# Attention scores in three rounded passes: queries, keys and rotary parts split into a high and a low part

## What is computed

```python
q = (rmsnorm(c_q, g_q) @ w_uq).reshape(B, T, N_HEADS, QK_NOPE + ROPE_DIM)
q_rope = rope(q[..., QK_NOPE:], pos)
k_rope = rope(k_r[:, :, None, :], pos)[:, :, 0, :]
q_lat = jnp.einsum('bthn,lhn->bthl', q_nope, w_uk)
s = (jnp.einsum('bqhl,bkl->bhqk', ql, ckv) + jnp.einsum('bqhr,bkr->bhqk', qr, krope))
p = jax.nn.softmax(jnp.where(mask, s * ATTN_SCALE, -jnp.inf), axis=-1)
```

## Time and profile before

| | us |
|---|---|
| median of 3 runs | 1477.38 |
| lowest, highest | 1475.58, 1477.49 |
| the profiled execution | 1478.73 |
| its span, first to last instruction | 1476.7 |
| TensorE busy / VectorE / ScalarE | 1283.9 / 532.7 / 457.6 |
| attention pairs, from the first scores | about 307.8 to 398 |
| granted TensorE clock, mean over the span | 0.937 |

### The profile page before, as it was taken

The page is one execution under the profiler, slowest core; times in us unless marked ns, Lnnn a source line. Parts: engine busy times, 40 slices in busy tenths (PEclk is TensorE's granted clock), DMA queues, the critical chain, the costliest instruction groups (busy, mean ns, idle before and its releaser), DMA issues.

```text
span 1476.7 us, 22967 instructions
## 1 busy us (share of the span) xinstructions
PE 1283.9 (87%) x8612; PEld 711.9 (48%) x8613; DVE 532.7 (36%) x1057; ACT 457.6 (31%) x713; POOL 32.9 (2%) x40
## 2 busy tenths in 40 slices
PE   6999999999999998888887788788788888888785
PEld 4999999887767753332232222222222323222222
DVE  4336446275574342322322232222223232232233
ACT  5432334245443223222222222222222322232223
POOL 1000000000100000000000000000000000000000
PEclk9999999999999989999899899889989989998988
DMA  9454551132354389999999999999999999999997
GB/s 325 142 171 139 167 168 41 36 109 78 118 163 150 134 340 393 428 430 433 430 435 431 430 432 430 436 430 432 432 429 402 424 433 432 429 436 430 433 431 287
DMA packets 70680, 474.45 MB, mean 321 GB/s; under 512 B 9628, under 2 KB 46752, under 8 KB 56432
## 3 DMA queue, kind: packets, MB, share of 16 engines
q1 hardware_dynamic: 69712, 472.35, 78.4%
q0 software_dynamic: 688, 1.43, 0.3%
q10 hardware_dynamic: 240, 0.09, 0.0%
HBM read 470.49 MB, written 3.38 MB: 321 GB/s over the span
## 4 chain that ended last, share of the span: by engine, by line
PE 63%; DMA 25%; DVE 6%; ACT 3%; issue 3%; DVEq 0%; ACTq 0%; SPq 0%
DMA ring<-in_w_down 14%; PE ps L955 11%; PE ps L974 8%; DMA ring<-in_w_up 7%; PE ps L653 5%; PE ps L655 5%; PE ps L654 5%; PE ps L929 3%; DVE hreg L1690 3%; PE ps L961 2%; DMA gate_b<-in_w_down 2%; DMA gate_b<-in_w_up 2%; PE ps L817 2%; PE ps L818 2%; PE ps L819 2%
## 5 line engine op out<-in xcount | busy, mean ns | idle before, releaser
L1690 DVE TENSOR_TENSOR hreg<-ps,hreg 128x512 f32<-128x512 f32 x264 | 160.9, 682 | 198.2 <-PE ps L981 198.2
L955 PE MATMUL ps<-ring,cq 128*32 128x512 f32 x1600 | 187.9, 611 | 24.9 <-DVE hreg L1690 18.4
L1694 DVE TENSOR_TENSOR work<-work,ps 128x128 f32 x33 | 9.5, 288 | 453.7 <-PE ps L961 453.7
L653 PE MATMUL ps<-xT_hi,w_hi 128*128 128x320 f32 (+1 forms) x528 | 165.2, 313 | 0.6 <-DVE w_lo L1395 0.6
L654 PE MATMUL ps<-xT_lo,w_hi 128*128 128x320 f32 (+1 forms) x528 | 164.2, 311 | 0.0
L655 PE MATMUL ps<-xT_hi,w_lo 128*128 128x320 f32 (+1 forms) x528 | 164.1, 311 | 0.0
L974 PE MATMUL ps<-ring,work 128*32 128x512 f32 x768 | 125.3, 812 | 18.5 <-DMA ring<-in_w_down 18.5
L981 PE MATMUL ps<-krt,const 32*128 32x512 f32 x528 | 102.7, 626 | 29.7 <-ACT krt L1341 29.7
L955 PEld LDWEIGHTS ps<-ring,cq 128*32 128x32 f32 x1600 | 52.0, 112 | 139.6 <-issue 129.0
L1395 DVE TENSOR_TENSOR w_lo<-ring,w_hi 128x1024 fp32r<-128x1024 f32 (+1 forms) x66 | 76.8, 1205 | 108.6 <-ACT w_hi L1091 108.6
L1091 ACT CAST w_hi<-ring 128x1024 fp32r<-128x1024 f32 (+1 forms) x66 | 65.2, 1033 | 146.8 <-PE ps L655 146.8
(11 more groups left out here) (306 smaller groups left out, 1650.9 us busy)
## 6 DMA issues: line engine op xcount, KB each, us to landing
ring<-in_w_up SPq DMA_DIRECT2D x23, 4096.0 KB, 31.8
ring<-in_w_down SPq DMA_DIRECT2D x23, 4096.0 KB, 32.7
ring<-in_w_gate SPq DMA_DIRECT2D x23, 4096.0 KB, 32.2
ring<-in_w_in SPq DMA_DIRECT2D x32, 1024.0 KB, 8.2
gate_b<-in_w_gate SPq DMA_DIRECT2D x8, 4096.0 KB, 31.0
gate_b<-in_w_up SPq DMA_DIRECT2D x8, 4096.0 KB, 31.8
gate_b<-in_w_down SPq DMA_DIRECT2D x7, 4096.0 KB, 33.1
ring<-in_w_o SPq DMA_DIRECT2D x16, 1024.0 KB, 7.2
```

The source lines that it names most:

```text
L653: pe.matmul(out, hi, xT_hi[:, c, :], start=c == 0, stop=False)
L955: last = pe.matmul(ps[r:r + B, bank, :], x[:, k % 4, k // 4, :], w[:, k, :], start=k < 4, stop=k >= KC - 4)
L1690: dve.tensor_tensor(h, ps[:, COMB_BANKS[u], :], h, ALU.add).then_inc(comb_added, 1)
```

## The change

Scores are formed in three fp32r passes, for the plain rows and for the rotary rows: six matmuls a step in place of two. Queries and keys get a high part (q_hi, k_hi; ScalarE copies) and a low part (q_lo, k_lo; VectorE subtractions), each in one buffer that all pairs use; the query banks are now emptied by VectorE, as the key banks already were. The rotary query is first rotated into att_a, then split (rope_hi_ready, rope_lo_ready). The rotary keys are split once, ahead of the pairs (krt_hi, krt_lo). Before its first pass of a pair, scores waits for rope_lo_ready. queries_hi(p+1) and keys_hi(p+1) move on ScalarE to behind the first key copy of pair p. In VectorE's keys(p), queries_lo(p+1) and keys_lo(p+1) keep their place, and the rotary subtraction stands behind them.

```diff
@@ psum_jobs @@
-        return ([(f"qr{p}", "act")] + [(f"q{2 * p + i}", "act") for i in range(2)]
+        return ([(f"qr{p}", "act")] + [(f"q{2 * p + i}", "dve") for i in range(2)]
@@ tensors @@
-        qt = r2[:, 0:1920].rearrange("p (b i t) -> p b i t", b=2, i=3)
-        kt = r2[:, 1920:4224].rearrange("p (b i k) -> p b i k", b=2, i=2)
+        q_hi = nc.alloc_sbuf_tensor_at("q_hi", [P, 3, T], F32R, offset=r2_at)
+        q_lo = nc.alloc_sbuf_tensor_at("q_lo", [P, 3, T], F32R, offset=r2_at + 4 * 960)
+        k_hi = nc.alloc_sbuf_tensor_at("k_hi", [P, 2, KEYS], F32R, offset=r2_at + 4 * 1920)
+        k_lo = nc.alloc_sbuf_tensor_at("k_lo", [P, 2, KEYS], F32R, offset=r2_at + 4 * 3072)
+        krt_hi = nc.alloc_sbuf_tensor_at("krt_hi", [P, KEYS], F32R, offset=work_at + 4 * 2560)
+        krt_lo = nc.alloc_sbuf_tensor_at("krt_lo", [P, KEYS], F32R, offset=krt_at)
@@ TensorE, scores(h) @@
-                q, k = qt[:, p % 2], kt[:, p % 2]
-                pe.wait_ge(q_ready, p + 1)
+                pe.wait_ge(krt_lo_ready, 1)
+                pe.wait_ge(rope_lo_ready, p + 1)
                 pe.wait_ge(drained["dve"], drain_count[f"K{h}_1"])
-                pe.wait_ge(drained["act"], drain_count[f"q{h}"])
+                rows = slice(64 * i, 64 * i + 64)
 
                 def score(out, t0, tn, k0, kn):
-                    pe.matmul(out, q[:, i, t0:t0 + tn], k[:, i, k0:k0 + kn], start=True, stop=False)
-                    return pe.matmul(out, q[64 * i:64 * i + 64, 2, t0:t0 + tn], krt[64 * i:64 * i + 64, k0:k0 + kn], start=False, stop=True)
+                    t, k = slice(t0, t0 + tn), slice(k0, k0 + kn)
+                    pe.matmul(out, q_hi[:, i, t], k_hi[:, i, k], start=True, stop=False)
+                    pe.matmul(out, q_hi[:, i, t], k_lo[:, i, k], start=False, stop=False)
+                    pe.matmul(out, q_lo[:, i, t], k_hi[:, i, k], start=False, stop=False)
+                    pe.matmul(out, q_hi[rows, 2, t], krt_hi[rows, k], start=False, stop=False)
+                    pe.matmul(out, q_hi[rows, 2, t], krt_lo[rows, k], start=False, stop=False)
+                    return pe.matmul(out, q_lo[rows, 2, t], krt_hi[rows, k], start=False, stop=True)
@@ ScalarE @@
             keys_hi(0)
+            act.wait_ge(ulast_ready, 1)
+            act.copy(krt_hi[:, :], krt[:, :]).then_inc(krt_hi_ready, 1)
...
                 for i in range(2):
                     act.wait_ge(psum_full, full(f"q{2 * p + i}"))
-                    drain("q", act.copy(qt[:, p % 2, i, :], bank(f"q{2 * p + i}")[:, 0:T]))
+                    act.copy(q_hi[:, i, :], bank(f"q{2 * p + i}")[:, 0:T]).then_inc(q_hi_ready, 1)
+                for i in range(2):
+                    for s, (k0, kn) in enumerate(((0, 256), (256, 320))):
+                        act.wait_ge(psum_full, full(f"K{2 * p + i}_{s}"))
+                        act.copy(k_hi[:, i, k0:k0 + kn], bank(f"K{2 * p + i}_{s}")[:, 0:kn]).then_inc(k_hi_ready, 1)
+                        if i == s == 0 and p + 1 < H // 2:
+                            queries_hi(p + 1)
+                            keys_hi(p + 1)
+                        if i == 0 and s == 1:
+                            act.wait_ge(q_ready, p + 1)
+                            act.copy(q_hi[:, 2, :], att_a).then_inc(rope_hi_ready, 1)
...
             queries(0)
-            queries_hi(1)
-            keys_hi(1)
...
-                if p + 2 < H // 2:
-                    queries_hi(p + 2)
-                    keys_hi(p + 2)
@@ VectorE @@
             keys_lo(0)
+            dve.wait_ge(krt_hi_ready, 1)
+            dve.tensor_tensor(krt_lo[:, :], krt[:, :], krt_hi[:, :].bitcast(F32), ALU.subtract).then_inc(krt_lo_ready, 1)
...
             def keys(p):
+                for i in range(2):
+                    h = 2 * p + i
+                    dve.wait_ge(q_hi_ready, h + 1)
+                    drain("q", dve.tensor_tensor(q_lo[:, i, :], bank(f"q{h}")[:, 0:T], q_hi[:, i, :].bitcast(F32), ALU.subtract))
                 for i in range(2):
                     for s, (k0, kn) in enumerate(((0, 256), (256, 320))):
                         name = f"K{2 * p + i}_{s}"
-                        dve.wait_ge(psum_full, full(name))
-                        drain(name, dve.tensor_copy(kt[:, p % 2, i, k0:k0 + kn], bank(name)[:, 0:kn]))
-                        if i == 0 and s == 1 and p + 1 < H // 2:
-                            queries_lo(p + 1)
-                            keys_lo(p + 1)
+                        dve.wait_ge(k_hi_ready, 4 * p + 2 * i + s + 1)
+                        drain(name, dve.tensor_tensor(k_lo[:, i, k0:k0 + kn], bank(name)[:, 0:kn], k_hi[:, i, k0:k0 + kn].bitcast(F32), ALU.subtract))
+                        if i == 0 and s == 1:
+                            if p + 1 < H // 2:
+                                queries_lo(p + 1)
+                                keys_lo(p + 1)
+                            dve.wait_ge(rope_hi_ready, p + 1)
+                            dve.tensor_tensor(q_lo[:, 2, :], att_a, q_hi[:, 2, :].bitcast(F32), ALU.subtract).then_inc(rope_lo_ready, 1)
                         if i == s == 0:
                             dve.wait_ge(drained["act"], drain_count[f"qr{p}"])
-                            rotate(qt[:, p % 2, 2, :], qraw, bank(f"qrot{p}")[:, 0:T], att_a, att_b, f"qrot{p}").then_inc(q_ready, 1)
+                            rotate(att_a, qraw, bank(f"qrot{p}")[:, 0:T], att_a, att_b, f"qrot{p}").then_inc(q_ready, 1)
```

More of the change, by code:

```diff
@@ L177, in trunk_layer_kernel @@
         cq = sb("cq", [P, LC, T])
+        krt_at = nc.sbuf_base
         krt = sb("krt", [P, KEYS])
+        assert nc.sbuf_base == krt_at + 4 * KEYS
         const = sb("const", [P, C_ALL])
@@ L182, in trunk_layer_kernel @@
         work = sb("work", [P, 4960])
+        work_at = nc.sbuf_base - 4 * 4960
         small = sb("small", [P, 64])
@@ L322, in trunk_layer_kernel @@
         wk_hi_ready, wk_lo_ready = sem("wk_hi_ready"), sem("wk_lo_ready")
+        q_hi_ready, k_hi_ready, rope_hi_ready, rope_lo_ready = sem("q_hi_ready"), sem("k_hi_ready"), sem("rope_hi_ready"), sem("rope_lo_ready")
+        krt_hi_ready, krt_lo_ready = sem("krt_hi_ready"), sem("krt_lo_ready")
         s_ones, first_half = sem("s_ones"), sem("first_half")
```

## The result

The changed kernel takes 1502.81 us (median of four runs, 1494.45 to 1508.86) against 1477.12 us for the kernel before (1475.58 to 1477.49): ratio 1.0175, 95% interval 1.0147 to 1.0202. It is slower, as forecast, but by 25.7 us and not by 6.2. The profiled execution took 1508.13 us (span 1506.1) against 1478.73 (span 1476.7): 29.4 us more.

A forecast was written before the change was run, and what follows sets the result against it. TensorE was taken to bound attention, passing delays on one for one. Terms 3.7 + 1.6 - 0.05 - 0.5 = +4.7 us, plus 1.5 for the clock, gave +6.2 us: 1483.6 us, range 1477.5 to 1489.5.

The forecast's parts named there:

- TensorE sets the pace of the stage, and a delay is passed on one for one: Attention stage: TensorE bounds it, VectorE close behind; any delay moves everything after it one for one.
- The worth of the passes, 0.5 us a pair: Scores on TensorE: three fp32r passes take 6.4 us a pair in place of 6.9, 2 us gained in all.
- 0.10 us of waiting plus an exposed load, 0.05 to 0.11: Score groups on TensorE: price of each change between 128 and 64 rows, six a head in both kernels.
- Rival B: Scores: row changes cost fp32r passes nothing, 4.6 us a pair, 1476.5 us in all; chance 0.10.
- rival D: Scores: narrow or 64-row fp32r passes run at f32 speed, +6 us more, about 1489 us; chance 0.05.
- The 1.8 us a head: Scores: estimate from the skill's issue-gap formula for six passes a step, set aside for 3.2 us a head.
- The first wait, 3.7 us: First pair: TensorE waits 3.7 us before the first scores for VectorE's added subtractions.
- Rival E: First scores: shorter or earlier side-engine work leaves a wait of 1 to 2 us, 1478 to 1481 us; chance 0.12.
- The gaps of pairs 1 and 2, +0.8 us a cycle, and pair 3: Before value matmuls: gaps of about 1.7 us, net +0.8 us for each of two cycles; third cycle net -0.05 us.
- rival A: Whole kernel: the clock doesn't fall, so only +4.7 us, 1482.1 us; chance 0.13.
- The clock, +1.5 us: First scores: one half-clock stretch of about 3.2 us follows TensorE's new wait and loses 1.5 us.
- Rival C: Pairs 1 and 2: clock also falls after one or both 1.7 us gaps, +1.6 us each, 1485 to 1487; chance 0.22.

The follow-up runs named there:

- experiment 1: Changed kernel with the first gap and the two gaps before attend filled by useless 512-column f32 matmuls on TensorE; 1482.60 us, ratio 1.0025.
- experiment 11: Changed kernel with the 1.7 us gaps filled, plus 24 fp32r passes of 256 columns in three forms before the first scores; 1483.84 us, one run.
- experiment 7: Kernel before with only its f32 score matmuls reordered, two changes of rows a head in place of six; 1474.67 us, ratio 0.9977.
- experiment 10: Changed kernel with 32 useless fp32r matmuls of 512 columns between the first gap and the first scores; 1503.68 us, ratio 1.0169.
- Experiment 8: Changed kernel with only the first gap, ahead of the first scores, filled by useless matmuls; 1498.26 us, ratio 1.0139.
- experiment 3: Changed kernel with next-pair weight casts behind the last key copy and weight subtractions behind the drains of transposed probabilities; 1478.78 us, ratio 1.0004.
- experiment 5: Changed kernel with the next pair's weight work moved later and score passes grouped to two changes of rows a head; 1469.97 us, ratio 0.9955.
- experiment 2: Changed kernel with each score step again two f32 matmuls, waits, splits and order kept; 1512.51 us, ratio 1.0219.
- experiment 6: Changed kernel with later weight work, grouped passes, and four of eight convolution scalings moved behind the first two heads' maxima; 1469.41 us, ratio 0.9946.
- experiment 4: Changed kernel with only its score passes reordered, two changes of rows a head in place of six; 1498.32 us, ratio 1.0117.

## Why the prediction was right, and where it failed

**TensorE sets the pace of the stage, and a delay is passed on one for one.** Right: 28.6 of 29.4 us are there when the output projection begins.

**The worth of the passes, 0.5 us a pair.** Right: 6.4 us for the last pair of the changed kernel, the only one at full clock, against 6.9. At full clock, in experiment 1, the groups of a head stand in the chain like this:

```profile
335.66 0.26 PE ps L778
...
337.16 0.32 PE ps L781
337.48 0.12 PE ps L782
337.59 0.12 PE ps L783
337.71 0.29 PE ps L778
338.00 0.15 PE ps L779
338.15 0.15 PE ps L780
...
338.88 0.26 PE ps L778
...
391.37 0.42 PE ps L831
```

The 256-column rotary group is 0.32 + 0.12 + 0.12 = 0.56 (forecast 0.56), the 320-column group behind it 0.29 + 0.15 + 0.15 = 0.59 (0.58), and a head, from 335.66 to 338.88, 3.22 us (3.2). The term "0.10 us of waiting plus an exposed load, 0.05 to 0.11" for a change of rows is 0.15 to 0.21, and experiment 11 measures 0.19. Rival B (changes cost passes nothing) falls by the same number, and rival D (narrow passes at f32 speed) by the groups. For the f32 matmuls of the kernel before, the prediction's reading was too simple: experiment 7 saves four changes a head and gains 0.40 us, 0.10 for each, not 0.20. The Trainium skill, TensorEngine Tiling (Array Packing), Key Properties, says that a changed tiling mode drains the engine; the trace agrees for rows (0.31 us against 0.12) and shows no such cost for weight columns from 128 to 64 (0.12 against 0.12). The 1.8 us a head that the prediction worked out from the Trainium skill, TensorE: Matmul & The Clock Gate, Back-to-back issue gap, is far off, but the page gives that formula for a matmul by itself and says that it counts too little for narrow ones in a stream with weight loads; the trace has 3.2 us with six changes of rows and 2.5 with two.

**The first wait, 3.7 us.** Right: 3.48. Of the single steps, the pair of query subtractions is 0.80 us to its successor in line (0.82) and the three of the weights 2.87 (2.87, 308.47 to 311.34). Rival E falls. (Its time was priced loosely: a wait of 1 to 2 us in place of 3.7 takes 1.7 to 2.7 us from 1483.6, and 1.5 more if the clock stays up, so 1479.4 at the lowest and not 1478.)

**The gaps of pairs 1 and 2, +0.8 us a cycle, and pair 3.** Right: 1.66 and 0.47 us of gap for 1.7 and 0.45. With the clock taken out the whole sum is +5.4 for +4.7 (interval 1.8 to 5.6). That is rival A's time (1482.1, measured 1482.60), but its condition, a clock that doesn't fall, holds only with the gaps filled.

**The clock, +1.5 us.** This is the step that failed, in both of its halves. It priced a fall of the clock from one case: "in two stretches of 2 us, so for 1.2 and 2.0 us, 3.2 us at least. The new wait of 3.7 us is longer, so I expect one such stretch". After the gap of the earlier trace rows TensorE went on with dense 512-column passes of the output projection; after the new gaps it goes on with scores or value matmuls. I carried over the length of the stretch and didn't ask what ended it. It is 13.7 to 20.5 us and not 3.2 to 3.4; experiment 10, with dense passes set behind the same gap, gets it down to some 6 us. And it left the 1.7 us gaps "out of the sum and in the range", priced in rival C at 1.6 us each. Experiment 8 shows that they act without the first gap, at about 8 us each. Rival C had the mechanism, and a fifth of its size.

The size follows from rows. From the first scores to the output projection are 104.3 us in the changed kernel (311.92 to 416.18) and 81.0 with the gaps filled (310.38 to 391.37): 23.3 us for 54.7 us of half clock, 0.43 us lost for each us. Half of a stretch would be lost if all its work followed the clock (256 columns: 0.21 against 0.12 us). The Trainium skill, TensorE: Matmul & The Clock Gate, Why this matters for your kernels, warns of idle gaps between bursts, but sets its limit above the gaps of pairs 1 and 2. By it, only the first gap would have mattered; the trace doesn't agree, with the clock at 0.50 behind 1.66 us.

**The range.** Its upper end came from rival D and from C at 1.6 us. With two or three falls at 7 to 8 us it would have had to reach 1505.

**What stays open.** A gap of a given length doesn't always bring the clock down. In experiment 3 the clock fell 2 us behind a wait of 0.82 us, and in experiment 5 it did not fall behind one of 0.83 us. The 2.14 us gap of the output projection did in the kernel before, and in the changed kernel, where it is as long, it did not:

```profile
436.00:446.00 10.00, 7.86 (x35) 6.19 (x34) 9.70 (x16) 5.08 (x8) 0.00 (x0) 1.00 0.77 146
```

The same gap of 2.14 us is in all fourteen profiles. The clock fell at it in five (the kernel before and experiments 1, 2, 6 and 7) and stayed full in the other nine. Experiments 5 and 6 have the same code ahead of the gap (16 matmuls of L853) and behind it (L840 to L842); it ends at 403.15 us in 5, where the clock is 1.00, and at 404.50 us in 6, where it is 0.50 from 405 to 408. So the work around the gap doesn't decide it here. The instant at which the gap falls may, but no run tested that by itself. The gaps of 1.66 or 1.67 us before the value matmuls had half clock in all twelve cases.

Nor did I find which property of scores and value matmuls keeps them from bringing the clock back. The number type alone is not it (experiment 2), nor is idle time as the profile counts it, since TensorE is busy all through. But the busy time of the scores has the 0.19 us for each change of rows in it, so they may well leave the array less to do than a dense stream; with four changes fewer a head the stretches were still 13.7, 17.1 and 20.5 us (experiment 4). A weight load before every pass is not enough by itself either: the queries and keys have that too, and the clock came back under them.

## What to carry to other kernels

When a change adds a wait to TensorE, price the wait, and then read what TensorE does behind it. If that is dense passes of 512 columns, half clock lasted 3 to 7 us here; if it is scores or value matmuls, it lasted 10 to 24 us, until the next pair's queries and keys had run for 2.5 to 5.8 us, and cost about 8 us for a gap of 1.7 (experiment 8), over four times its own length. Before giving up on such a change, look at which of the new steps on the side engines is needed next: here the same arithmetic in another order took the cost away, and with grouped rows it is 8.0 us faster than the kernel before (5.3 us faster than experiment 7, the kernel before with the same grouping).

## What the runs showed that I had not expected

- Half clock is entered at every idle time of 1.7 us, at one of 2.14 us in five profiles of fourteen, and once 2 us behind one of 0.8 us.
- The same scores run at 1.00 for their whole length in experiments 1, 5, 6 and 10, and at 0.50 for nearly their whole length behind a gap; in no profile did the clock come back under them. In experiment 3 it fell under them.
- A change between 128 and 64 rows costs 0.19 us for fp32r passes, more than a whole 256-column pass (0.12); a change between 128 and 64 weight columns costs them nothing. For f32 matmuls a head with four changes of rows fewer gains only 0.40 us.
- Useless matmuls in three gaps made the changed kernel 20 us faster.
